# A two-layer decoder trunk on one NeuronCore: the normalised x handed over in PSUM, the query remainders one unit later, the compressed softmax without clamps, the sliding values among the first score units

## The chip, the cores and the metric

The kernel runs on one core of one Trainium2 chip. The metric is the device time of one execution in microseconds (us). A core has a matrix engine (PE), a vector engine (DVE), a scalar engine (ACT), a general engine (POOL) and a queue for DMA (SP), which run side by side and wait for each other on semaphores. PE writes its results to PSUM, which has eight banks of 128 x 512 numbers of 4 bytes; DVE and ACT read and write PSUM and SBUF.

## What is computed

`x` is 512 tokens by 1024 features. Two layers run, each of four sub-layers, and every sub-layer ends in a LayerNorm, so there are eight of them (`ln` 0 to 7 in the code):

```
for i in range(2):
    x = layer_norm(DN_ALPHA * x + 0.5 * swiglu(x, ffn1_gate[i], ffn1_up[i], ffn1_down[i]))
    y = swa_mixer(x, ...) if i == 0 else nsa_mixer(x, ...)
    x = layer_norm(DN_ALPHA * x + y)
    x = layer_norm(DN_ALPHA * x + mem_cross_attention(x, mem, ...))
    x = layer_norm(DN_ALPHA * x + 0.5 * swiglu(x, ffn2_gate[i], ffn2_up[i], ffn2_down[i]))
```

`swa_mixer` is attention of 16 heads over a sliding window of 128 tokens, with a learned sink for each head. `nsa_mixer` adds three attentions, each times a gate: one over 31 compressed blocks of keys, one over selected blocks (with these sizes all of the causal past), one over a window (also all of it). In the compressed one a token that no block precedes has probability 0 everywhere:

```
s_c = einsum('bsgrd,bngd->bgrsn', q, k_cmp) - slopes * dist_c
p_c = where(valid_c, softmax(where(valid_c, s_c, NEG_INF)), 0.0)
o_cmp = einsum('bgrsn,bngd->bsgrd', p_c, v_cmp)
```

## The kernel before

**Arithmetic.** Every product is made of three matmuls on numbers split in a rounded part and a remainder: `x_hi*w_hi`, `x_lo*w_hi`, `x_hi*w_lo` (L1328 to L1330). A slab is 128 output columns of a weight: DMA brings it to `w_raw`, ACT rounds it to `w_hi` (L621), POOL takes the remainder `w_lo` (L461). There are 379 slabs in four slots, so ACT rounds slab s when PE is done with slab s-4. ACT and POOL each have one queue in program order; calls of `feed` place the slabs in it.

**The norm between two sub-layers.** `t` holds the eight chunks (128 features by 512 tokens) of the sum. For chunk j DVE subtracts the mean (`centre`, L1024), multiplies by gain and 1/std (`scale`, L1043, out to `t`), ACT adds the offset and rounds to `x_hi` (L729), and DVE takes the remainder `x_lo` from `t` and `x_hi` (`lo`, L1049). DVE's order is scale(j), lo(j-1), centre(j+1). Norms 2, 3 and 6 (`KEEPS`) leave `lo` to POOL. Meanwhile PE projects the memory for the cross attention: `FILL` gives a norm groups of one or two of these slabs, each group into one of banks 5 and 7; norms 0, 1 and 5 have five groups, the others two, three or none. After chunk j for j in `FILL_BEHIND` (by default 1, 3, 5) ACT rounds the next slabs and copies a finished group out (L700, L704), and DVE takes that group's remainder. The next sub-layer begins with `alone` (L1372: the eight `x_hi` chunks times `w_hi`) or `together`.

**The mixers.** Heads come in eight pairs p. A unit is one head's scores for one tile of 128 queries; a pair has 8 units in the sliding mixer and 17 in the other (8 selected, 1 compressed, 8 window). In one loop over the unit number n each engine does its share for the units in flight: PE the scores of unit n (L1591, L1592), some chunks of the next pair's query slab into bank 7, transposes of finished probabilities (`turn`, L1619) and the products with the values (`values`, L1658); DVE the bias and the row minimum (`biased`, L1247; for the compressed unit the chain L1222 to L1228), the reciprocals two units later (`recip`, L1195 to L1210) and copies of turned probabilities to `pf` (L1263); ACT the exponentials (L881), the other copies to `pf` (L758), and the rounding of the next pair's queries (`q_round`, L765); POOL the normalisation (L564). DVE's `q_rest` (L1125) takes the query remainders behind `q_round`, both at the unit that `q_done` names: unit 3 of a pair in the sliding mixer, in the other 13 (14 in the first pair). PE starts the scores of unit n only when `add` counts n-2 units, and a new pair only when `qlo` says that its queries' remainders are there. `turn` m is copied by ACT if `on_act(m)`, here for even m; a pair of the second mixer has 13 turns, so from pair to pair the two engines change roles.

**The start of the sliding mixer.** PE makes two key slabs, the first query slab and then the values of all four token tiles (96 matmuls of 256 columns, L1423 to L1425, banks 5 and 6), and only then the first scores.

Of the kernel before, what the change touches and what calls it, by code (L numbers as in the profile page):

```python
# [13 lines left out]
P = 128  # L14
# [13 lines left out]
MASKED = -1.0e34  # L28
SLOTS = 4
# [40 lines left out]
class Stage:  # L70


    def __init__(self, kind, layer, ln):
# [24 lines left out]
class Mixer:  # L98
# [145 lines left out]
def build(nc, io):  # L244
# [4 lines left out]
    with ExitStack() as ctx:  # L249
# [201 lines left out]
        def _(pool):  # L451
# [24 lines left out]
            def masks():  # L476
# [51 lines left out]
            def mixer(st):  # L528
# [14 lines left out]
                for n in range(M.n + 1):  # L543
# [68 lines left out]
        def _(act):  # L612
# [77 lines left out]
            def norm(st):  # L690
# [32 lines left out]
                for j in range(KC):  # L723
# [4 lines left out]
                    else:  # L728
                        act.activation(x_hi[:, j, :], t[:, j, :], ACT.Identity, bias=b).then_inc(xhi_ready, 1)  # L729
# [44 lines left out]
            def mixer(st):  # L774
                z, M = st.sem, mixers[st.kind]
                sl = st.slab
                if st.kind == "swa":
                    feed(sl["v1"])
                    for c in range(2):
                        act.wait_ge(slab_done, sl[f"ks{c}"] + 1)  # L780
                        for half in range(2):
# [45 lines left out]
                act.wait_ge(dist_ready, 4)  # L827
                for n in range(M.end):
# [5 lines left out]
                    if st.kind == "nsa" and n in TOKENS:  # L834
                        values_nsa(st, TOKENS[n])
# [3 lines left out]
                    p = M.q_done(n)  # L839
                    if p is not None:  # L840
# [99 lines left out]
        def _(dve):  # L940
# [80 lines left out]
            def norm(st):  # L1021
# [16 lines left out]
                def scale(j):  # L1038
# [4 lines left out]
                    dve.scalar_tensor_tensor(out=t[:, j, :], in0=t[:, j, :], scalar=lng[:, st.ln, j:j + 1],  # L1043
# [879 lines left out]
```

## Time and profile before

| | us |
|---|---|
| median of 3 runs | 2307.63 (2306.52 to 2309.23) |
| the profiled execution | 2303.9 |
| its span in the trace | 2302.1 |
| PE busy in the span | 2243.1 |
| DVE, ACT, POOL busy | 732.5, 840.6, 1122.6 |

All times of the trace count from the start of the span. A row of the timeline is: start in us, duration in us, engine, line, operation with output<-input, count, and in brackets how long the engine had been idle before it and what ended that. DMA, ACT and DVE have large idle shares and are not what sets the time. The trace has its granted PE clock at 1.00 (2.4 GHz) nearly everywhere and at 0.50 (1.2 GHz) in a few short stretches.

### The profile page before, as it was taken

The numbers are of one execution on the slowest core, as the hardware profiler recorded it, in microseconds if no ns is written. First come the engines' busy times: TensorE is split into PE (matmuls) and PEld (weight loads), VectorE is DVE, ScalarE is ACT, GpSimd is POOL, SyncE is SP. The second block draws the span as 40 slices with busy tenths as digits, with TensorE's granted clock in tenths as the row PEclk, the third lists the DMA queues.
The fourth block names the chain that finished last, engine by engine and source line by source line (L and its number), as shares of the span: only waits on it lengthen the run. The fifth ranks groups of instructions, "written<-read, shape, count | busy, mean of one in ns | idle before, by whom it ended". The sixth has DMA issues, their size and how long they took to land.

```text
span 2302.1 us, 27948 instructions
## 1 busy us (share of the span) xinstructions
PE 2243.1 (97%) x10918; PEld 1846.0 (80%) x10918; DVE 732.5 (32%) x1499; ACT 840.6 (37%) x1433; POOL 1122.6 (49%) x698
## 2 busy tenths in 40 slices
PE   9999999999999999999999999999999999999998
PEld 7888888777888888888888888776667888888886
DVE  2111126564435111114211112656654444111115
ACT  3322224553435222223422223456653444222223
POOL 5454445447537444444644444444547546444443
PEclk9999999999999999999999999999999999999999
DMA  5332324213413333333333232310003313232331
GB/s 188 99 97 92 104 75 131 70 38 101 131 44 101 116 94 97 97 96 95 101 96 96 92 101 83 101 56 19 28 11 112 112 42 99 94 101 93 100 95 61
DMA packets 57874, 204.91 MB, mean 89 GB/s; under 512 B 6928, under 2 KB 7056, under 8 KB 57232
## 3 DMA queue, kind: packets, MB, share of 16 engines
q1 hardware_dynamic: 56016, 197.68, 27.3%
q10 hardware_dynamic: 1728, 5.45, 0.7%
q8 instruction: 87, 1.43, 0.3%
q14 instruction: 43, 0.35, 0.0%
HBM read 201.01 MB, written 2.10 MB: 88 GB/s over the span
## 4 chain that ended last, share of the span: by engine, by line
PE 91%; DVE 4%; ACT 2%; issue 2%; POOL 1%; DMA 0%; ACTq 0%; DVEq 0%
PE bank L1328 25%; PE bank L1330 25%; PE bank L1329 25%; PE bank L1658 2%; PE bank L1619 1%; PE bank L1591 1%; PE bank L1423 1%; DVE x_lo L1049 1%; PE bank L1358 1%; PE bank L1425 1%; PE bank L1424 1%; PE bank L1592 1%; PE bank L1347 1%; POOL w_lo L461 1%; PE bank L1355 1%
## 5 line engine op out<-in xcount | busy, mean ns | idle before, releaser
L461 POOL TENSOR_TENSOR w_lo<-w_raw,w_hi 128x1024 fp32r<-128x1024 f32 (+1 forms) x378 | 895.2, 2372 | 912.8 <-ACT w_hi L621 912.4
L1328 PE MATMUL bank<-x_hi,w_hi 128*128 128x512 f32 x1568 | 612.5, 391 | 0.0
L1329 PE MATMUL bank<-x_lo,w_hi 128*128 128x512 f32 x1568 | 610.9, 390 | 0.0
L1330 PE MATMUL bank<-x_hi,w_lo 128*128 128x512 f32 x1568 | 610.6, 389 | 0.0
L621 ACT ACTIVATE w_hi<-w_raw 128x1024 fp32r<-128x1024 f32 (+1 forms) x379 | 391.1, 1036 | 515.0 <-PE bank L1330 492.5
L1328 PE MATMUL bank<-h_hi,w_hi 128*128 128x512 f32 x960 | 379.7, 396 | 3.9 <-DVE h_lo L1270 2.8
L1330 PE MATMUL bank<-h_hi,w_lo 128*128 128x512 f32 x960 | 373.9, 389 | 0.0
L1329 PE MATMUL bank<-h_lo,w_hi 128*128 128x512 f32 x960 | 373.8, 389 | 0.0
L1330 PEld LDWEIGHTS bank<-x_hi,w_lo 128*128 128x128 f32 x1568 | 294.6, 188 | 61.8
L1329 PEld LDWEIGHTS bank<-x_lo,w_hi 128*128 128x128 f32 x1568 | 294.8, 188 | 58.5
L1328 PEld LDWEIGHTS bank<-x_hi,w_hi 128*128 128x128 f32 x1568 | 294.7, 188 | 58.4
L1098 DVE SCALAR_TENSOR_TENSOR f<-f,bank 128x512 f32<-128x512 f32 x88 | 60.6, 688 | 834.2 <-PE bank L1330 802.2
L1328 PEld LDWEIGHTS bank<-h_hi,w_hi 128*128 128x128 f32 x960 | 180.2, 188 | 47.5 <-issue 4.5
L1329 PEld LDWEIGHTS bank<-h_lo,w_hi 128*128 128x128 f32 x960 | 180.3, 188 | 37.9 <-issue 1.9
L1330 PEld LDWEIGHTS bank<-h_hi,w_lo 128*128 128x128 f32 x960 | 180.2, 188 | 37.7
L657 ACT ACTIVATE f<-bank 128x512 f32<-128x512 f32 x88 | 52.6, 597 | 361.2 <-PE bank L1330 344.6
L688 ACT ACTIVATE f<-t 128x512 f32<-128x512 f32 x64 | 40.4, 632 | 179.5 <-DVE t L999 127.4
L1247 DVE CUSTOM_DVE_ANT_0 f<-bank,dist 128x512 f32<-128x512 f32 (+3 forms) x128 | 61.2, 487 | 38.3 <-PE bank L1592 37.1
L662 ACT ACTIVATE h_hi<-f 128x512 fp32r<-128x512 f32 x88 | 54.7, 622 | 50.7 <-DVE f L1098 50.7
L881 ACT ACTIVATE t<-f,small 128x257 f32<-128x257 f32 (+5 forms) x104 | 55.1, 531 | 48.9 <-DVE small L1247 48.3
L1658 PE MATMUL bank<-pf,f 128*64 128x256 f32 (+3 forms) x384 | 61.4, 425 | 11.9 <-DVE pf L1263 6.9
L564 POOL TENSOR_SCALAR t<-t,small,gates 128x512 f32<-128x512 f32 (+3 forms) x68 | 40.8, 608 | 64.1 <-DVE small L1210 64.1
(235 smaller groups left out, 2493.0 us busy)
## 6 DMA issues: line engine op xcount, KB each, us to landing
w_raw<-w_dram SPq DMA_DIRECT2D x315, 512.0 KB, 3.5
w_raw<-w_dram SPq DMA_DIRECT2D x64, 448.0 KB, 3.2
f<-mem_dram ACTq DMA_DIRECT2D x3, 1024.0 KB, 4.9
out_dram<-t SPq DMA_DIRECT2D x8, 256.0 KB, 2.2
t<-x_dram SPq DMA_DIRECT2D x2, 512.0 KB, 6.8
f<-cmp_w_dram ACTq DMA_DIRECT2D x1, 1024.0 KB, 8.7
t<-x_dram ACTq DMA_DIRECT2D x2, 256.0 KB, 5.4
t<-x_dram ACTq DMA_DIRECT2D x1, 512.0 KB, 8.1
```

The lines of the kernel that those rows point to most:

```text
L461: pool.tensor_tensor(w_lo[:, slot(s), 0:n * P], w_raw[:, s % RAW, 0:n * P], w_hi[:, slot(s), 0:n * P].bitcast(F32), ALU.subtract).then_inc ...
L564: pool.tensor_scalar(pr, pr, rinv[:, c:c + 1], gates[:, u.i, col:col + 1], ALU.mult, ALU.mult).then_inc(z["pn"], 1)
L621: act.activation(w_hi[:, slot(s), 0:n * P], w_raw[:, s % RAW, 0:n * P], ACT.Copy).then_inc(hi_ready, 1)
L657: act.activation(gated[pair % 2], bank[UP_BANK[2 * pair % 4]][:], ACT.Silu).then_inc(z["gated"], 1)
L662: act.activation(h_hi[:, n, :], hidden[pair % 2], ACT.Copy).then_inc(z["hhi"], 1)
L881: act.activation(prob_of(u)[:, at0 - sink:at0 + u.width], scores_at(M, u)[:, 0:u.width + sink], ACT.Exp, bias=negm[:, c:c + 1], scale=-1.0 ...
L1098: dve.scalar_tensor_tensor(out=hidden[pair % 2], in0=gated[pair % 2], scalar=0.5, in1=bank[UP_BANK[(2 * pair + 1) % 4]][:], op0=ALU.mult, ...
L1247: dve.tensor_tensor_reduce(dst, src[:, 0:w], bias, -slope(h), first, ALU.add, ALU.min, negm[:, c:c + 1]).then_inc(z["add"], 1)
L1328: pe.matmul(dst, w_hi[:, slot(s), w], m_hi[:, k, :], start=k == 0, stop=False)
L1329: pe.matmul(dst, w_hi[:, slot(s), w], m_lo[:, k, :], start=False, stop=False)
L1330: last = pe.matmul(dst, w_lo[:, slot(s), w], m_hi[:, k, :], start=False, stop=k == n - 1)
L1658: last = pe.matmul(o, vals[:, b, j, rows], probs, start=begin and n < 2, stop=end and n >= len(parts) - 2, skip_group_check=True)
```

## The change

1. **x through PSUM in the full norms.** In the norms with five groups of fill (0, 1 and 5) `scale` writes to banks 6 and 4 in turn instead of `t`, and both `x_hi` and `lo` read there. `FILL_BEHIND` becomes (1, 3) for norm 1 and (1, 4) for norm 5.
2. **Queries.** `q_done` becomes `q_rounded` (ACT) and `q_rest` (DVE). In the sliding mixer ACT rounds at unit 3 as before and DVE takes the remainder at unit 4; in the first pair 5 and 6. In the other mixer they stand at 12 and 14, in the first pair at 13 and 15.
3. **`on_act`** counts turns within a pair (`m % 13 % 2 == 0`), so every pair has the same split.
4. **The compressed chain** loses both clamps (L1226, L1198). Instead the 32nd, unused column of its bias is set to -1e29. Its sum stays in PSUM, and POOL multiplies by the gates instead of DVE (L1202).
5. **Sliding values.** Tile 0 of the values stands before unit 0 and tiles 1, 2, 3 behind the scores of units 0, 1, 2, in banks 0 and 1. The next query slab's chunks move two units later in the first pair.

```diff
-FILL_BEHIND = {1: (1, 4), 5: (3, 6)}
+FILL_BEHIND = {1: (1, 3), 5: (1, 4)}
+X_BANK = (6, 4)
-TOKENS = {1: 2, 3: 3}
+TOKENS = {"swa": {0: 1, 1: 2, 2: 3}, "nsa": {1: 2, 3: 3}}
+    def x_at(self, t, bank, j):
+        return bank[X_BANK[j % 2]][:] if len(self.fill) == 5 else t[:, j, :]
...
-        return self.kind == "nsa" and m % 2 == 0
+        return self.kind == "nsa" and m % 13 % 2 == 0
...
-                at = b + k // 2 if self.kind == "swa" else b + (5 + k if p == 0 else 1 + 3 * k // 2)
+                at = (b + 2 + k // 2 if p == 0 else b + k // 2) if self.kind == "swa" else b + (5 + k if p == 0 else 1 + 3 * k // 2)
...
-            if n == self.base[p] + (3 if self.kind == "swa" else 14 if p == 0 else 13):
...
+    def q_rounded(self, n):
+        at = {"swa": (5, 3), "nsa": (13, 12)}[self.kind]
+        return [p + 1 for p in range(7) if n == self.base[p] + at[p > 0]]
+    def q_rest(self, n):
+        at = {"swa": (6, 4), "nsa": (15, 14)}[self.kind]
...
+                pool.memset(cd[:, :, NCMP:NCMP + 1], EMPTY).then_inc(dist_ready, 1)
...
                     if u.br == "cmp":
+                        pool.tensor_tensor(r8.rearrange("p (a b h) -> p a b h", a=2, b=2),
+                                           q8.rearrange("p (a b h) -> p a b h", a=2, b=2),
+                                           gates[:, :, 2 * u.p:2 * u.p + 2].rearrange("p (b a) h -> p a b h", a=2),
+                                           ALU.mult).then_inc(z["gated"], 1)
+                        pool.wait_ge(z["gated"], u.p + 1)
...
-                        act.activation(x_hi[:, j, :], t[:, j, :], ACT.Identity, bias=b).then_inc(xhi_ready, 1)
+                        act.activation(x_hi[:, j, :], st.x_at(t, bank, j), ACT.Identity, bias=b).then_inc(xhi_ready, 1)
...
-                    feed(sl["q1"])
-                    act.wait_ge(slab_done, sl["v1"] + 1)
-                    act.activation(vals[:, :, 0:2, :].rearrange("p b i d -> p i b d"),
-                                   bank[5][:].rearrange("p (i b d) -> p i b d", i=2, b=2), ACT.Copy).then_inc(z["vhi"], 1)
-                    feed(sl["q2"] + 1)
+                    feed(sl["q2"])
...
+                    if st.kind == "swa" and n == max(TOKENS["swa"]):
+                        act.wait_ge(slab_done, sl["v1"] + 1)
+                        act.activation(vals[:, :, 0:2, :].rearrange("p b i d -> p i b d"),
+                                       bank[0][:].rearrange("p (i b d) -> p i b d", i=2, b=2), ACT.Copy).then_inc(z["vhi"], 1)
...
-                    dve.scalar_tensor_tensor(out=t[:, j, :], in0=t[:, j, :], scalar=lng[:, st.ln, j:j + 1],
+                    dve.scalar_tensor_tensor(out=st.x_at(t, bank, j), in0=t[:, j, :], scalar=lng[:, st.ln, j:j + 1],
...
-                    dve.scalar_tensor_tensor(out=x_lo[:, j, :], in0=t[:, j, :], scalar=lnb[:, st.ln, j:j + 1],
+                    dve.scalar_tensor_tensor(out=x_lo[:, j, :], in0=st.x_at(t, bank, j), scalar=lnb[:, st.ln, j:j + 1],
...
-                        link(dve.tensor_scalar(s8, s8, 1.0e-30, None, ALU.max))
-                        link(dve.reciprocal(q8, s8))
+                        dve.reciprocal(q8, s8).then_inc(z["rinv"], 1)
...
-                        link(dve.tensor_tensor(sc, both[:, 1], sc, ALU.add))
+                        link(dve.tensor_tensor(both[:, 0], both[:, 1], sc, ALU.add))
-                        link(dve.tensor_scalar(m8, m8, -1.0e29, None, ALU.max))
...
-                elif u.n and st.kind == "swa":
-                    pe.wait_ge(z[("vhi", "vlo")[u.n - 1]], 1)
```

The order in three places, names as in the code; `ISA` with `dist` is `biased`, and numbers at tiles are bank numbers. First PE at the start of the sliding mixer: the end of the values' matmuls, the first scores (`mv` holds the keys, `h_hi` and `h_lo` the queries) and the first chunk of the next query slab (bank 7).

```order
L1424 MATMUL bank6<-w_hi,x_lo 128x256
L1425 MATMUL bank6<-w_lo,x_hi 128x256
L1591 MATMUL bank4<-mv,h_hi 128x256
L1592 MATMUL bank4<-mv,h_hi 128x256
L1328 MATMUL bank7<-x_hi,w_hi 128x512
```

After, the end of tile 0 of the values, the first scores, and the beginning of tile 1:

```order
L1434 MATMUL bank0<-w_lo,x_hi 128x256
L1598 MATMUL bank4<-mv,h_hi 128x256
L1599 MATMUL bank4<-mv,h_hi 128x256
L1432 MATMUL bank0<-w_hi,x_hi 128x256
L1433 MATMUL bank0<-w_hi,x_lo 128x256
```

So 72 matmuls of the values moved from ahead of the first scores to between the first three and what follows. Second, DVE at units 3 to 5 of a pair of the sliding mixer, before:

```order
L1210 RECIPROCAL small<-small 128x2
L1263 COPY pf<-bank2 128x512
L1125 SCALAR_TENSOR_TENSOR h_hi<-bank7,h_hi 64x512
L1125 SCALAR_TENSOR_TENSOR h_lo<-bank7,h_lo 64x512
L1247 ISA f2,small<-bank6,dist,nsinks 128x256
L1247 ISA small 128x1
L1247 ISA f2,small<-bank4,dist,nsinks 128x256
L1247 ISA small 128x1
L1210 RECIPROCAL small<-small 128x2
L1263 COPY pf<-bank3 128x512
```

and after:

```order
L1218 RECIPROCAL small<-small 128x2
L1269 COPY pf<-bank2 128x512
L1253 ISA f2,small<-bank6,dist,nsinks 128x256
L1253 ISA small 128x1
L1141 SCALAR_TENSOR_TENSOR h_hi<-bank7,h_hi 64x512
L1141 SCALAR_TENSOR_TENSOR h_lo<-bank7,h_lo 64x512
L1253 ISA f2,small<-bank4,dist,nsinks 128x256
L1253 ISA small 128x1
L1218 RECIPROCAL small<-small 128x2
L1269 COPY pf<-bank3 128x512
```

The bias of unit 4 went ahead of the two query remainders; both copies to `pf` stay around them. Third, DVE at units 13 to 15 of a pair of the other mixer, before:

```order
L1247 ISA f2,small<-bank6,dist 128x256
L1247 ISA small 128x1
L1125 SCALAR_TENSOR_TENSOR h_hi<-bank7,h_hi 64x512
L1125 SCALAR_TENSOR_TENSOR h_lo<-bank7,h_lo 64x512
L1247 ISA f2,small<-bank4,dist 128x256
L1247 ISA small 128x1
L1210 RECIPROCAL small<-small 128x2
L1247 ISA f2,small<-bank5,dist 128x128
```

and after:

```order
L1253 ISA f2,small<-bank6,dist 128x256
L1253 ISA small 128x1
L1253 ISA f2,small<-bank4,dist 128x256
L1253 ISA small 128x1
L1218 RECIPROCAL small<-small 128x2
L1141 SCALAR_TENSOR_TENSOR h_hi<-bank7,h_hi 64x512
L1141 SCALAR_TENSOR_TENSOR h_lo<-bank7,h_lo 64x512
L1253 ISA f2,small<-bank5,dist 128x128
```

Here unit 14's bias and a reciprocal went ahead of the remainders, while on ACT the rounding went ahead of unit 13's exponential.

## Rows read from the trace of the kernel before

**Rows 1.** The page, part 1: busy time, share of the span, instructions.

```profile
PE 2243.1 (97%) x10918; PEld 1846.0 (80%) x10918; DVE 732.5 (32%) x1499; ACT 840.6 (37%) x1433; POOL 1122.6 (49%) x698
```

**Rows 2.** Waits of PE: who waited for whom, us in total, times, longest.

```profile
PE bank L1591 <- DVE small L1247: 12.0, 13, 2.2
PE bank L1423 <- POOL w_lo L461: 9.8, 4, 4.9
PE bank L1658 <- DVE pf L1263: 6.9, 11, 1.2
PE bank L1372 <- ACT x_hi L729: 3.1, 1, 3.1
```

**Rows 3.** Windows: stretch, length, busy by engine (PE, PEld, DVE, ACT, POOL), PEclk, DMA.

```profile
397.20:400.00 2.80, 2.77 (x12) 2.31 (x13) 1.13 (x3) 1.20 (x2) 1.52 (x1) 1.00 0.69 181
434.50:436.50 2.00, 2.00 (x6) 1.61 (x6) 1.18 (x7) 1.36 (x6) 2.00 (x4) 0.50 1.02 238
1534.60:1538.00 3.40, 3.40 (x20) 2.23 (x20) 2.32 (x11) 2.99 (x10) 2.37 (x2) 0.65 0.41 148
1793.50:1796.00 2.50, 2.42 (x11) 2.45 (x12) 2.46 (x5) 0.94 (x2) 0.00 (x0) 0.50 0.62 177
```

**Rows 4.** Single lines of DVE: count, duration in ns as min/median/max, first and last start.

```profile
L1043 DVE SCALAR_TENSOR_TENSOR t<-t,lng,bank x64: 730/748/750, 375.4 to 2297.9; 128x512 f32<-128x512 f32 x64
L1125 DVE SCALAR_TENSOR_TENSOR h_hi<-bank,h_hi x16: 683/684/687, 412.9 to 1692.3; 64x512 fp32r<-64x512 f32 x16
```

**Rows 5.** Groups by line of DVE, norm 0 (377 to 398.5): count | busy, mean ns | idle.

```profile
L1049 DVE SCALAR_TENSOR_TENSOR x_lo<-t,lnb,x_hi 128x512 fp32r<-128x512 f32 x8 | 11.6, 1464 | 0.0
```

**Rows 6.** Timeline of norm 0: DVE, POOL, PE.

```profile
385.21 2.77 DVE L1049 SCALAR_TENSOR_TENSOR x_lo<-t,lnb,x_hi 128x512 fp32r<-128x512 f32 x1
385.03 5.21 POOL L461 TENSOR_TENSOR w_lo<-w_raw,w_hi 128x1024 fp32r<-128x1024 f32 x2 [3.92 <-ACT w_hi L621]
397.23 0.50 PE L1372 MATMUL bank<-x_hi,w_hi 128*128 128x512 f32 x1 [3.10 <-ACT x_hi L729]
```

**Rows 7.** Timeline of norms 1 and 5: ACT's rounding, and PE behind it.

```profile
587.54 1.99 ACT L621 ACTIVATE w_hi<-w_raw 128x1024 fp32r<-128x1024 f32 x2
593.98 0.55 PE L1423 MATMUL bank<-w_hi,ra 128*128 128x256 f32 x1 [2.90 <-POOL w_lo L461]
...
1787.21 1.99 ACT L621 ACTIVATE w_hi<-w_raw 128x1024 fp32r<-128x1024 f32 x2
1793.58 0.55 PE L1423 MATMUL bank<-w_hi,ra 128*128 128x256 f32 x1 [4.88 <-POOL w_lo L461]
```

**Rows 8.** Timeline of PE in the first pair of the sliding mixer.

```profile
433.15 0.48 PE L1591 MATMUL bank<-mv,h_lo 128*128 128x128 f32 x1 [2.24 <-DVE small L1247]
```

**Rows 9.** Timeline of a later pair of the sliding mixer, DVE and PE.

```profile
480.38 0.69 DVE L1263 COPY pf<-bank 128x512 f32<-128x512 f32 x1 [1.26 <-PE bank L1619]
...
483.09 0.33 PE L1591 MATMUL bank<-mv,h_lo 128*128 128x128 f32 x1 [0.67 <-DVE small L1247]
...
484.25 0.62 PE L1658 MATMUL bank<-pf,f 128*64 128x256 f32 x3 [0.48 <-DVE pf L1263]
```

**Rows 10.** Timeline of the other mixer's first pair: DVE, POOL, PE.

```profile
1531.08 2.38 DVE L1198 TENSOR_SCALAR small<-small 128x8 f32<-128x8 f32 x1
1531.07 2.36 POOL L461 TENSOR_TENSOR w_lo<-w_raw,w_hi 128x1024 fp32r<-128x1024 f32 x1
1534.60 0.44 PE L1658 MATMUL bank<-pf,f 128*64 128x128 f32 x4 [2.06 <-issue]
```

**Rows 11.** Timeline of two later pairs of the other mixer: PE, ACT, DVE.

```profile
1618.93 0.65 PE L1658 MATMUL bank<-pf,f 128*64 128x512 f32 x2 [1.16 <-DVE pf L1263]
...
1640.25 0.58 ACT L765 ACTIVATE h_hi<-bank 64x512 fp32r<-64x512 f32 x1
1640.86 0.68 DVE L1125 SCALAR_TENSOR_TENSOR h_hi<-bank,h_hi 64x512 fp32r<-64x512 f32 x1 [1.21 <-ACT h_hi L765]
1644.05 0.65 PE L1658 MATMUL bank<-pf,f 128*64 128x512 f32 x2 [0.31 <-ACT pf L758]
```

More of the change, by code:

```diff
@@ L28 @@
 MASKED = -1.0e34
+EMPTY = -1.0e29
 SLOTS = 4
@@ L198, in q_chunks @@
         return out
-    def q_done(self, n):
-        for p in range(7):
-            if n == self.base[p] + (3 if self.kind == "swa" else 14 if p == 0 else 13):
-                return p + 1
-        return None
+    def q_rounded(self, n):
[3 more added lines that the diff above has]
+        at = {"swa": (6, 4), "nsa": (15, 14)}[self.kind]
+        return [p + 1 for p in range(7) if n == self.base[p] + at[p > 0]]
 def kv_order(kind):
@@ L838, in mixer @@
                     turned(st, M, n)
-                    p = M.q_done(n)
-                    if p is not None:
+                    for p in M.q_rounded(n):
                         act.wait_ge(slab_done, sl[f"q{p}"] + 1)
@@ L1149, in mixer @@
                     q_rest(st, M, 0, bank[FIRST_BANK[2]])
-                    dve.wait_ge(slab_done, st.slab["v1"] + 1)
-                    dve.tensor_copy(vals[:, :, 2:4, :].rearrange("p b i d -> p i b d"),
-                                    bank[6][:].rearrange("p (i b d) -> p i b d", i=2, b=2)).then_inc(z["vlo"], 1)
                 else:
@@ L1252, in mixer @@
                         biased(M.units[n])
-                    if st.kind == "nsa" and n - 3 in TOKENS:
-                        gate(TOKENS[n - 3])
+                    if st.kind == "nsa" and n - 3 in TOKENS["nsa"]:
+                        gate(TOKENS["nsa"][n - 3])
                     if 2 <= n < M.n + 2:
@@ L1263, in mixer @@
                             dve.tensor_copy(pf[:, tn.m % 4, 0:w], bank[M.t_bank(tn.m)][:, 0:w]).then_inc(z["td"], 1)
-                    p = M.q_done(n)
-                    if p is not None:
+                    if st.kind == "swa" and n == max(TOKENS["swa"]):
+                        dve.wait_ge(slab_done, st.slab["v1"] + 1)
+                        dve.tensor_copy(vals[:, :, 2:4, :].rearrange("p b i d -> p i b d"),
+                                        bank[1][:].rearrange("p (i b d) -> p i b d", i=2, b=2)).then_inc(z["vlo"], 1)
+                    for p in M.q_rest(n):
                         q_rest(st, M, p, bank[Q_BANK])
@@ L1669, in mixer @@
                     wait_lo(pe, sl["v1"])
-                    for i in range(NT):
-                        b = bank[(5, 6)[i // 2]][:, 256 * (i % 2):256 * (i % 2) + 256]
-                        last = token_major([sl["v0"], sl["v1"]], b, i, x_hi, x_lo, 256)
-                    last.then_inc(slab_done, 2)
+                    tokens(st, 0)
                 else:
@@ L1704, in mixer @@
                         scores(st, M, M.units[n])
-                    if st.kind == "nsa" and n in TOKENS:
-                        tokens(st, TOKENS[n])
+                    if n in TOKENS[st.kind]:
+                        tokens(st, TOKENS[st.kind][n])
                     for p, k in M.q_chunks(n):
@@ L1732, in tokens @@
                 sl = st.slab
+                if st.kind == "swa":
+                    last = token_major([sl["v0"], sl["v1"]], bank[k // 2][:, 256 * (k % 2):256 * (k % 2) + 256], k, x_hi, x_lo,
+                                       256)
+                    if k == NT - 1:
+                        last.then_inc(slab_done, 2)
+                    return
                 last = token_major([sl["vs"], sl["vw"], sl["gl"]], bank[(7, 0, 1, 2)[k]][:, 0:384], NT - 1 - k, x_hi, x_lo,
```

19 lines of the change are left out of this document (7 added, 12 removed).

## The prediction

> **What bounds the kernel.** The page first: PE is busy for 2243.1 of 2302.1 us [rows 1], so at most 59 us can be won by removing waits, and some 14 of them lie at the start, the end, in the other norms and at the mixers' ends, which the change leaves alone. No engine but PE is near its limit; DVE, ACT and POOL matter only where PE stands still for them. So the second view is the list of PE's own waits [rows 2]: for the scores behind DVE's bias 12.0 us in 13 waits, for the fill slabs in the norms behind POOL's remainders 9.8 in 4, for value products behind copies to `pf` 6.9 in 11, and one of 3.1 for the last `x_hi`. The third view is the granted clock in windows [rows 3]: behind some waits it stands at 0.50 (1.2 GHz). Behind waits of 2.05 [rows 10], 2.24 [rows 8] and 4.88 [rows 7] it fell, behind one of 3.10 [rows 6] it did not (1.00 from 397.2 on), so a wait near 2 us may or may not bring the low clock. A low stretch costs half its length in matmuls.
>
> **Part 1, x through PSUM.** Every `lo` of the full norms reads two tiles of SBUF. In norm 0 the eight take 1464 ns in the mean [rows 5], and the one of 2.77 us lies inside POOL's 5.21 us for two slabs [rows 6]: it waits for POOL. DVE instructions of the same kind with one input from PSUM never take more than 750 ns (`scale`, 64 times) or 687 (`q_rest`) [rows 4], though POOL works half the time. The change gives `lo` a PSUM input, so I take 0.75 for each. Norm 0 then has 8 x (1.46 - 0.75) = 5.7 us less on DVE. PE waits there 3.10 for the last `x_hi` [rows 6]. Counting the chain again (scale, lo, centre, about 2.1 us a chunk, plus ACT's two roundings where it has to wait for a slot) the last `x_hi` comes near 392.9, about 1 us before PE asks for it: **-3.3** with 0.2 from the remainder of a fill group that DVE then has ready. Next late there is POOL's remainder of the first key slab, near 388, which leaves room.
>
> In norms 1 and 5 PE waits 2.90 and 4.88 us for POOL [rows 7], and POOL for ACT, which rounds the pair of slabs only behind `x_hi` of chunk 4 (norm 1, at 587.54) and chunk 3 (norm 5, at 1787.21). Their slots were free at 584.3 and 1783.0, when PE had ended the group before. `FILL_BEHIND` asks for them after chunks 3 and 1, and without DVE's stalls these chunks are done in time. So in norm 1 ACT rounds at 584.3, POOL is done at 1.1 + 4.8 later, 590.2, when PE ends the group in between; of 2.90 and a wait of 0.84 before it some 0.4 is left: -3.3, and the low clock behind it (2.9 us long, half lost) goes: -1.4, **-4.6** with rounding down. In norm 5 ACT rounds at 1783.0, POOL is done at 1788.9 where PE asks at 1788.7: -4.6, and the low clock (0.50 at 1793.5 to 1796 [rows 3], 4.7 us of it in all) gives 2.2: **-6.8**. Next late is `x_hi` of chunk 7, near 593.0 and 1796.3, 3 and 1 us before PE needs it. What hides the new reads and writes in banks 4 and 6 is that `together` and `alone` write them only after the last `x_lo`.
>
> One page speaks against this part. The Trainium skill ("VectorE: DVE Perf Modes", the section on the TRN2 errata) gives a VectorE instruction 58 fixed cycles from SBUF and 120 from PSUM; at its 0.96 GHz that is 65 ns more, 1.6 us over 24 `lo`, estimated from that page. The trace does not agree: 0.69 us with a PSUM input against 0.75 [rows 4], though over half the partitions.
>
> **Part 5, the sliding mixer's start.** Before, the scores of the first nine units come within 11 us, and PE stands 2.24 us for DVE's bias behind `q_rest` [rows 8]; the clock is 0.50 after it [rows 3]. After, three units have 2.9 us of value matmuls between them, so ACT's table load, its exponentials and the biases are long done. The chunks of the next query slab end at unit 5, ACT rounds them (2 x 0.6) and DVE takes the remainders (2 x 0.7), and the scores of unit 8 wait for these: about 1.4 us instead of 2.2. That is -0.8, and -1.6 for a low stretch of 3.4 us that ends: **-2.4**. The first query remainders are ready 0.7 us before tile 0 of the values ends, so unit 0 does not wait. If the low clock stays, it is -0.8.
>
> **Part 2 in the sliding mixer.** Here the step costs. In each later pair, PE's value products wait for the copy of unit 5 [rows 9]. Before that copy DVE does, without a pause: copy of unit 3 (at 480.38), two remainders, bias 4, bias 5, reciprocal, copy; PE goes on at 484.25. After, bias 4 stands behind the first copy, and its scores end only at 481.6, 0.5 us after the copy, since PE has value products ahead of them. DVE idles for that and does the same work afterwards: 484.25 becomes 484.8. PE's wait of 0.67 for unit 7's scores goes, but only into the wait for the copy. Six pairs have it: 6 x 0.53 = **+3.2**. The bounds are 0, if something else in that chain has slack that I don't see, and 6 x 0.7.
>
> **Parts 2, 3 and 4 in the other mixer.** First pair: both clamps wait for POOL, one of them 2.38 us beside a remainder of 2.36 [rows 10]; behind it the copy comes late, PE waits 2.05, and the clock is 0.65 in the mean over the next 3.4 us [rows 3]. The clamps go; the reductions and reciprocals that stay lie in the same trace at their usual length. But now `q_rest` stands at unit 15 behind a copy that waits for PE's turn of that unit: the next pair's scores wait some 2.0 us. Balance, worked out from 1534.60 to the value products after the first scores of the next pair, which took 8.6 us with the wait and take 3.9 + 2.0 + 1.0 now: **-1.7**. If the clock falls behind that wait too, for which the rows of 2.05 and 2.24 speak and the one of 3.10 doesn't, it is 0.
>
> Later pairs: at the border to the next pair PE waits for bias 14 behind `q_rest`, which itself waited 1.21 us for ACT's rounding [rows 11]. After that it waits for the copies of turns 14 and 15. Where DVE had turn 14 and ACT turn 15, the four waits are 0.2, 0.2, 0.9 and 1.16; where it was the other way round, 1.0 and 0.31 [rows 11]. The change gives every pair the second split. It puts the rounding behind exponential 12, so it starts at 1639.76 instead of 1640.25, and bias 14 no longer queues. DVE ends the remainders at 1641.8, just when PE ends unit 16; ACT ends its copy at 1642.4, DVE the other at 1642.7. PE's value products go from 1644.05 to 1642.95: -1.1 in three pairs. In the other three it is 2.5 - 0.2 = 2.3, and 0.4 in the last: 3.3 + 6.9 + 0.4 = **-10.6**. POOL's extra multiply by the gates has no row; the nearest are 0.17 for it on DVE and 0.6 for the 256-wide one behind it, and its user on PE comes 9 us later, so 0. Were it not covered, 8 x 0.6 would be +4.8.
>
> **Sum.** -3.3 - 4.6 - 6.8 - 2.4 + 3.2 - 1.7 - 10.6 = -26.2. The profiled execution of 2303.9 (span 2302.1) becomes 2277.7; on the median of 2307.6, 3.7 above it, **2281.4**.
>
> **The rivals.** (A) The hand-over doesn't free DVE: `lo` still waits for POOL. Against it speaks that 80 instructions with a PSUM input show no such wait [rows 4]. Norm 0 gives nothing, norms 1 and 5 keep what the earlier rounding brings (2.2 + 1.4, 4.2 + 2.2 less some stalls, about 9): sum -20.5, 2287. By the page's 65 ns it would be 1.6 more.
> (B) The merged wait in the sliding pairs, 0.67 + 0.48 + 0.53 = 1.7, brings the low clock in each: 6 x 1.7 = +10.2, 2291.6. For it: the clock fell behind 2.05. Against: it did not behind 3.10, nor behind 1.4.
> (C) In the second mixer the border wait only changes its cause, because the copies on ACT come later than I counted behind the rounding. Then only the equal split helps, 3 x 1.2 + 0.4 = 4: -19.6, 2288.
> (D) Slower: the late `q_rest` is a loss at every border. In the second mixer it holds up DVE's copy of turn 15 as it does in the first, +0.53 in place of the gain, and the wait grows over the point where the clock falls. Then the mixers give -2.4 + 3.2 - 1.7 + 3.2 and 12 x 1.7 = 20.4, the norms -14.7: +8, 2315.6. It decides from waits of about 2 us at all twelve borders; the two places in the trace with such waits lost the clock each time.
>
> **How the numbers follow.** Forecast 0.65, (A) 0.07, (B) 0.11, (C) 0.12, (D) 0.05. All but (D) are faster by more than 4.6 us (0.2%, about what a measurement of this kernel tells from no change); I give no change 0.02 out of the forecast's unknowns. The forecast alone spans 2277 (no loss in the sliding pairs, then 2278) to 2286 (the low clock back in both first pairs, +3.3). The range runs from 2275 to 2293: it takes in A, B and C.
>
> **What would show it.** In the changed profile: `x_lo` of the full norms at 0.7 to 0.8 us each and no wait of 3.1 before `alone`; PE's waits for POOL in norms 1 and 5 under 0.5; clock 1.00 in all three norms; the value products of each sliding pair behind one wait near 1.7 where two of 0.67 and 0.48 stood; no DVE instruction of 1.5 to 2.4 in the compressed chain; the borders of the second mixer's pairs under 0.4, except the first near 2.0. The sum is wrong if sliding pairs don't grow from 12.5 us, or if the second mixer's don't shrink to about 24.0 each where they now take 25.1 and 26.3 in turn.

## The result, and the profile after

The changed kernel takes 2283.91 us (median of 4 runs, 2281.93 to 2285.78), the kernel before 2307.16 beside it (4 runs, 2306.52 to 2309.23): a ratio of 0.9898 (95%: 0.988 to 0.9915), so it takes 1.0% less time. The forecast was 2281.4, the range 2275 to 2293. The profiled execution took 2284.9, with a span of 2283.1. Its page, part 1, answers [rows 1]:

```profile
PE 2242.0 (98%) x10918; PEld 1846.9 (81%) x10918; DVE 708.8 (31%) x1471; ACT 843.4 (37%) x1437; POOL 1121.9 (49%) x707
```

PE does the same 10918 matmuls in about the same busy time (1.1 us less). The span is 19.0 us shorter, and PE's idle time in it fell from 59.0 to 41.1 us, by 17.9. PE's waits, as in [rows 2] (total, times, longest):

```profile
PE bank L1665 <- DVE pf L1269: 12.3, 7, 2.0
PE bank L1598 <- issue: 3.6, 2, 2.1
...
PE bank L1432 <- POOL w_lo L472: 1.9, 3, 1.1
```

L1665 is now the products with the values, L1598 the scores, L1432 the fill and the sliding values. `issue` means that the profile names nothing that ended the wait; by the order of the code the two long ones at L1598, each ahead of a second pair's first scores, are for the query remainders. The 12.0 us for the bias, the 3.1 for `x_hi` and most of the 9.8 for POOL have gone; what stands for `pf` has grown from 6.9 to 12.3, nearly all of it six waits of 1.99 in the sliding pairs. No DVE instruction of the compressed chain takes over 1.2 us now, where the two clamps took 1.5 and 2.4. The single lines of `lo` (min/median/max in ns) belong beside [rows 4, 5]; the second row is norm 4, which still goes through `t`:

```profile
L1065 DVE SCALAR_TENSOR_TENSOR x_lo<-bank,lnb,x_hi x24: 744/746/751, 378.9 to 1783.9; 128x512 fp32r<-128x512 f32 x24
L1065 DVE SCALAR_TENSOR_TENSOR x_lo<-t,lnb,x_hi x8: 737/747/2181, 1465.3 to 1480.1; 128x512 fp32r<-128x512 f32 x8
```

The timeline (start, duration, then in brackets the idle time ahead and its cause) shows, from above: the products of `alone` in norm 0, all eight without the wait of [rows 6], the first sliding pair [rows 8], four later ones [rows 9], norm 1 [rows 7], the second mixer's first scores, its first border [rows 10] and two later ones [rows 11], norm 5 [rows 7].

```profile
393.20 2.03 PE L1381 MATMUL bank<-x_hi,w_hi 128*128 128x512 f32 x8
...
430.39 0.36 PE L1598 MATMUL bank<-mv,h_hi 128*128 128x256 f32 x1 [1.53 <-issue]
...
442.53 1.63 PE L1665 MATMUL bank<-pf,f 128*64 128x256 f32 x8 [1.99 <-DVE pf L1269]
...
457.28 1.09 PE L1665 MATMUL bank<-pf,f 128*64 128x256 f32 x8 [1.99 <-DVE pf L1269]
...
470.44 1.98 PE L1665 MATMUL bank<-pf,f 128*64 128x256 f32 x8 [1.99 <-DVE pf L1269]
...
485.10 1.08 PE L1665 MATMUL bank<-pf,f 128*64 128x256 f32 x8 [1.99 <-DVE pf L1269]
...
586.79 0.36 PE L1432 MATMUL bank<-w_hi,ra 128*128 128x256 f32 x1 [0.41 <-POOL w_lo L472]
...
1512.11 0.39 PE L1598 MATMUL bank<-mv,h_hi 128*128 128x512 f32 x1
...
1538.30 0.49 PE L1598 MATMUL bank<-mv,h_hi 128*128 128x512 f32 x1 [2.10 <-issue]
...
1563.56 0.47 PE L1598 MATMUL bank<-mv,h_hi 128*128 128x512 f32 x1
...
1611.16 0.47 PE L1598 MATMUL bank<-mv,h_hi 128*128 128x512 f32 x1
...
1776.73 0.36 PE L1432 MATMUL bank<-w_hi,ra 128*128 128x256 f32 x1 [0.35 <-POOL w_lo L472]
```

Last the granted clock in windows (columns as in [rows 3]; the seventh figure without brackets, ahead of the DMA share, is PEclk), at five places where it fell:

```profile
442.50:446.00 3.50, 3.47 (x14) 2.31 (x15) 1.47 (x9) 1.23 (x5) 1.58 (x3) 0.56 0.19 74
469.80:473.50 3.70, 3.06 (x12) 1.92 (x13) 1.72 (x9) 1.35 (x6) 2.18 (x4) 0.56 0.27 109
1470.00:1473.40 3.40, 3.40 (x10) 2.63 (x9) 3.37 (x7) 0.92 (x2) 0.00 (x0) 0.55 0.55 151
1501.20:1504.50 3.30, 3.04 (x10) 3.04 (x10) 0.00 (x0) 1.09 (x3) 0.21 (x1) 0.50 0.53 154
1538.30:1542.00 3.70, 3.70 (x9) 1.49 (x10) 1.00 (x5) 1.58 (x5) 1.09 (x2) 0.54 0.21 83
```

The third and the fourth lie behind norm 4, at the start of the second mixer, which no part of the change touches. At the same two places the clock of the kernel before was at its full level:

```profile
1473.00:1476.00 3.00, 3.00 (x14) 2.23 (x13) 2.96 (x6) 0.76 (x2) 0.00 (x0) 1.00 0.41 164
1503.00:1506.00 3.00, 3.00 (x18) 3.00 (x19) 0.00 (x0) 0.72 (x3) 0.00 (x0) 1.00 0.54 178
```

To compare kernels I cut the profiled executions at one landmark, the first matmul with `ones` in which PE sums up `t` for a norm's mean. "First mixer" runs from norm 0 to norm 1 and holds norm 0 and the sliding mixer, "norm 1" from there to norm 2, "second mixer" from norm 4 to norm 5 (with norm 4), "norm 5" from there to norm 6. Behind the slash stand the stretches of low clock in the stage, a long one counted as two.

| kernel | time, us | first mixer | norm 1 | second mixer | norm 5 |
|---|---|---|---|---|---|
| before | 2303.9 (profile) | 198.8 / 1 | 149.0 / 1 | 309.6 / 1 | 150.8 / 2 |
| changed | 2284.9 (profile) | 199.4 / 2 | 144.1 / 0 | 300.1 / 3 | 144.1 / 0 |
| e3_psum_only | 2296.2 | 193.2 / 0 | 144.8 / 0 | 311.0 / 1 | 150.1 / 2 |
| e4_fill_only | 2300.7 | 201.5 / 3 | 146.4 / 0 | 309.5 / 1 | 146.6 / 0 |
| e2_part1 | 2292.7 median | 194.9 / 1 | 144.1 / 0 | 312.5 / 3 | 144.1 / 0 |
| e1_rest3 | 2276.9 median | 192.6 / 0 | 144.1 / 0 | 299.0 / 2 | 144.1 / 0 |
| e6_swalate | 2313.7 median | 207.3 / 4 | 148.9 / 1 | 309.6 / 1 | 150.8 / 2 |
| e5_clamps | 2308.2 | 200.4 / 2 | 149.0 / 1 | 310.1 / 2 | 150.6 / 2 |
| e5_onact | 2304.1 | 200.4 / 2 | 148.9 / 1 | 305.9 / 1 | 150.9 / 2 |
| e7_nsaq | 2302.1 | 201.5 / 3 | 149.2 / 1 | 303.9 / 2 | 150.7 / 2 |
| e9_nsaq_onact | 2296.2 | 200.4 / 2 | 149.1 / 1 | 298.6 / 1 | 151.1 / 2 |
| e8_best | 2273.5 median | 192.5 / 0 | 144.1 / 0 | 294.6 / 0 | 144.1 / 0 |

One low stretch is worth up to 1.7 us: e2_part1 and e3_psum_only have the same first mixer but for one, 194.9 against 193.2. At other places it costs less. Behind the four waits of 1.99 where the clock fell (two in the changed kernel, two in e6_swalate) the pair takes 14.66 to 14.76 us instead of 13.17, so 1.5 to 1.6. At the start of the second mixer, from the landmark of norm 4 to the first scores, it is 82.4 to 82.5 us in the eight profiles without a low stretch, 83.8 and 84.1 in e7_nsaq and e1_rest3 with one, and 85.2 in e2_part1 and the changed kernel with two: 1.4 to 1.6 each, 2.7 for two.

### The profile page after: what moved, and what is told of

Read it like the earlier page. It is cut to its first block, busy times and chain, and to the rows that moved or that the text cites. A ratio compares the mean times of both kernels' runs of the same rounds, so it can differ in the third digit from the quotient of the medians.

```text
span 2283.1 us, 27932 instructions
## 1 busy us (share of the span) xinstructions
PE 2242.0 (98%) x10918; PEld 1846.9 (81%) x10918; DVE 708.8 (31%) x1471; ACT 843.4 (37%) x1437; POOL 1121.9 (49%) x707
## 3 DMA queue, kind: packets, MB, share of 16 engines
q8 instruction: 87, 1.43, 0.3%
## 4 chain that ended last, share of the span: by engine, by line
PE 94%; DVE 2%; issue 2%; ACT 1%; POOL 1%; DMA 0%; ACTq 0%; DVEq 0%
PE bank L1337 26%; PE bank L1339 26%; PE bank L1338 26%; PE bank L1665 2%; PE bank L1626 1%; PE bank L1598 1%; PE bank L1599 1%; PE bank L1432 1%; PE bank L1433 1%; PE bank L1434 1%; PE bank L1367 1%; PE bank L1356 1%; POOL w_lo L472 1%; PE bank L1364 1%; PE bank L1371 0%
## 5 line engine op out<-in xcount | busy, mean ns | idle before, releaser
L1665 PE MATMUL bank<-pf,f 128*64 128x256 f32 (+3 forms) x384 | 63.1, 435 | 12.5 <-DVE pf L1269 12.3
```

Of the source, the lines that this page charges most:

```text
L1665: last = pe.matmul(o, vals[:, b, j, rows], probs, start=begin and n < 2, stop=end and n >= len(parts) - 2, skip_group_check=True)
```

## Experiments

### Part 1 whole, and its two halves

e2_part1 is the kernel before with the hand-over in PSUM and the new `FILL_BEHIND`; e3_psum_only has the first of these edits, e4_fill_only the second.

```diff
+        return bank[X_BANK[j % 2]][:] if len(self.fill) == 5 else t[:, j, :]
-FILL_BEHIND = {1: (1, 4), 5: (3, 6)}
+FILL_BEHIND = {1: (1, 3), 5: (1, 4)}
```

> The kernel before with part 1 alone (x through PSUM in the full norms and the earlier rounding of fill slabs). My theory: -3.3 us in norm 0, -4.6 in norm 1, -6.8 in norm 5, the rest of the kernel as before: 2307.2 - 14.7 = 2292.5 us, with x_lo at 0.7 to 0.8 us each and no granted clock of 0.50 in these norms. Rival: part of what the three norms gain in the changed kernel is due to other parts (the clock, or work that arrives shifted from the mixers); then norm 1 or norm 5 gains less here than there.

> The kernel before with x through PSUM in the full norms, and the rounding of the fill slabs left where it was. My theory: norm 0 gains 3.3 us. In norm 1 the chunk that the rounding stands behind (4) is done 2 us earlier without DVE's stalls, which gives most of the 4.6, 4. In norm 5 it stands behind chunk 3, which only one stall of 0.25 us held up, so PE's wait of 4.88 becomes 4.3 and the clock still falls: -0.6. Sum -8, 2299. Rival: the hand-over through PSUM alone gives all, -14.7 (the places of the rounding are idle), or nothing in norms 1 and 5 (-3.3).

> The kernel before with the rounding of the fill slabs moved ahead (behind chunks 1 and 3 in norm 1, 1 and 4 in norm 5), and x in SBUF as before. My theory: norm 0 unchanged with its wait of 3.1. Norm 1: the rounding starts when chunk 3 is done, 585.3 instead of 587.5, so the wait of 2.90 falls to about 0.7: -2.2, and -1.4 if the clock then stays up. Norm 5: the rounding starts at 1783.0, the wait of 4.88 goes to 0.7 or less and the clock stays up: -6.3. Sum -9 to -10, 2298. Rival: the earlier rounding puts POOL's remainders beside more of DVE's x_lo, the stalls eat the gain, and less than half of it, 4, is left.

Measured: 2292.73 for the whole (4 runs, ratio 0.994, 0.9925 to 0.9955, beside a median of 2306.29), 2296.21 and 2300.69 in one run each. DVE's group in norm 0 (count, busy, mean ns), first e3_psum_only, then e4_fill_only:

```profile
L1054 DVE SCALAR_TENSOR_TENSOR x_lo<-bank,lnb,x_hi 128x512 fp32r<-128x512 f32 x8 | 6.0, 745 | 0.1
```

```profile
L1049 DVE SCALAR_TENSOR_TENSOR x_lo<-t,lnb,x_hi 128x512 fp32r<-128x512 f32 x8 | 11.7, 1466 | 0.0
```

So it is the PSUM input, and nothing else of the change, that frees `lo` of POOL; with it goes PE's wait of 3.10 in norm 0. In norms 1 and 5 the halves are not a plain sum. Timeline of e3_psum_only, norms 1 and 5:

```profile
586.89 0.36 PE L1428 MATMUL bank<-w_hi,ra 128*128 128x256 f32 x1 [0.54 <-POOL w_lo L466]
...
1785.82 0.55 PE L1428 MATMUL bank<-w_hi,ra 128*128 128x256 f32 x1 [4.15 <-POOL w_lo L466]
```

and of e4_fill_only, norm 0 and norm 5 (L1066 is DVE's remainder of a fill group):

```profile
398.23 0.79 PE L1372 MATMUL bank<-x_hi,w_hi 128*128 128x512 f32 x1 [3.10 <-ACT x_hi L729]
...
1790.50 0.36 PE L1423 MATMUL bank<-w_hi,ra 128*128 128x256 f32 x1 [0.77 <-POOL w_lo L461]
1798.28 0.39 PE L1328 MATMUL bank<-ra,w_hi 128*128 128x256 f32 x1 [1.80 <-DVE mv L1066]
```

In norm 1 the hand-over alone takes 4.1 of the 4.8 us: DVE is at chunk 4 in time, and the earlier rounding has little left to give. In norm 5 it takes 0.6 alone, since ACT still rounds behind chunk 3; the new `FILL_BEHIND` takes 4.2 alone and then PE waits 1.80 for DVE, which had stood at a `lo` of 2.78 us (at 1794.25) beside POOL's 5.18 for two slabs; together they take 6.7. Of the earlier rounding alone 2.2 to 3.6 us were expected in norm 1 and 6.3 in norm 5; it gave 2.5 and 4.2. So the stalls eat a part of its gain, as the rival said, but 6.7 us of the 9 to 10 are left, where the rival left 4. Its 2300.69 also holds three low stretches in the first mixer, where the profile of before has one. For e2_part1 the rival was that other parts of the change had helped in these norms. It is excluded: norms 1 and 5 take 144.1 us each in e2_part1 as in the changed kernel.

### The sliding mixer's remainders: put back, and moved alone

e1_rest3 is the changed kernel with one number back; e6_swalate is the kernel before with that one move.

```diff
-        at = {"swa": (6, 4), "nsa": (15, 14)}[self.kind]
+        at = {"swa": (6, 3), "nsa": (15, 14)}[self.kind]
```

> The changed kernel with one number put back: from the second pair of the sliding mixer on, DVE takes the query remainders at unit 3 again, not 4. My theory: the later place costs PE 0.63 us in each of six pairs (pairs of 13.17 us instead of 12.54) and makes one wait of 1.99 out of two of 0.67 and 0.48. So this kernel is 3.8 us faster than the changed one by the waits, 2280 us, and up to 3.4 more where the granted clock had fallen behind the waits of 1.99; PE's longest wait in these pairs is under 0.8 us and the clock there is 1.00. Rival: the 1.99 come from the values moved among the first units or from another part, and the place of the remainders changes nothing; then it stays at 2284 with waits of 1.99.

> The kernel before, and only the sliding mixer's later pairs take their query remainders at unit 4 instead of 3. Theory: this one move makes the six longer pairs of the changed kernel; the two waits of 0.67 and 0.48 become one of 1.99 and each pair grows by 0.63: +3.8. The clock falls behind some of them (in the changed kernel behind 2 of 6), 1.7 us each: +3.4. Together 2306.3 + 7.2 = 2313.5, 2310 without a fall. Rival: the longer pairs come from the values' new places or from the mixer's start; then the pairs stay at 12.54 us and the time at 2306.

Measured: 2276.90 (4 runs, 0.9873, 0.9857 to 0.989), 7.0 under the changed kernel (6.1 if each is measured from the kernel before that ran beside it, 2306.29 and 2307.16); and 2313.69 (10 runs, 2310.8 to 2314.68; 1.0027, 1.0017 to 1.0036), 6.8 over the kernel before, where 7.2 were expected. The rival for e6_swalate, that the long pairs come from the values' new places, is excluded. e1_rest3 has the two short waits of [rows 9] back:

```profile
453.02 0.33 PE L1598 MATMUL bank<-mv,h_lo 128*128 128x128 f32 x1 [0.66 <-DVE small L1253]
454.17 1.08 PE L1665 MATMUL bank<-pf,f 128*64 128x256 f32 x8 [0.48 <-DVE pf L1269]
```

e6_swalate has one of 1.99 in each of the six pairs; behind the first the clock stayed up, behind the second it fell (timeline, then windows):

```profile
450.17 1.08 PE L1659 MATMUL bank<-pf,f 128*64 128x256 f32 x8 [1.99 <-DVE pf L1265]
463.33 1.98 PE L1659 MATMUL bank<-pf,f 128*64 128x256 f32 x8 [1.99 <-DVE pf L1265]
```

```profile
450.20:453.40 3.20, 3.20 (x20) 2.42 (x21) 1.40 (x9) 1.82 (x7) 1.52 (x3) 1.00 0.19 72
463.70:467.00 3.30, 3.30 (x14) 2.06 (x11) 1.06 (x7) 0.88 (x5) 1.18 (x3) 0.54 0.07 29
```

DVE there, in the same pair of e6_swalate:

```profile
445.66 0.69 DVE L1265 COPY pf<-bank 128x512 f32<-128x512 f32 x1 [1.24 <-PE bank L1620]
446.90 0.48 DVE L1249 CUSTOM_DVE_ANT_0 f<-bank,dist,nsinks 128x256 f32<-128x256 f32 x1 [0.55 <-PE bank L1593]
...
447.43 0.68 DVE L1127 SCALAR_TENSOR_TENSOR h_hi<-bank,h_hi 64x512 fp32r<-64x512 f32 x1
...
449.35 0.67 DVE L1265 COPY pf<-bank 128x512 f32<-128x512 f32 x1
```

This is the loss as the prediction told it: 0.55 us in which DVE stands for bias 4's scores with the remainders queued behind it. The two kernels agree on the price: six pairs at 0.63 and two low stretches at 1.5 make 6.8.

### The second mixer, part by part

e5_clamps has part 4 alone on the kernel before, e5_onact part 3, e7_nsaq the later pairs' new units of part 2, e9_nsaq_onact the last two together.

```diff
+                pool.memset(cd[:, :, NCMP:NCMP + 1], EMPTY).then_inc(dist_ready, 1)
-                        link(dve.tensor_scalar(s8, s8, 1.0e-30, None, ALU.max))
-                        link(dve.tensor_scalar(m8, m8, -1.0e29, None, ALU.max))
```

```diff
-        return self.kind == "nsa" and m % 2 == 0
+        return self.kind == "nsa" and m % 13 % 2 == 0
```

```diff
+    def q_rounded(self, n):
+        at = {"swa": (3, 3), "nsa": (14, 12)}[self.kind]
+    def q_rest(self, n):
+        at = {"swa": (3, 3), "nsa": (14, 14)}[self.kind]
```

> The kernel before, and only the compressed chain changed: no clamps, the 32nd column's bias at -1e29, the gates multiplied on POOL. Theory: only the 2.05 us in the first pair go (no clamp waits for POOL any more), with the low clock behind them (1.7); the border behind, which waited 0.42 at the low clock and 1.57 in e3_psum_only at the full one, waits 1.6: -2.6 against the profiled execution before, 2301.3 to 2303.7. Rival: POOL's multiply by the gates holds up the products with the compressed values in every pair: +4.8, 2308 to 2311.

> The kernel before, and only the turns counted within a pair, so that ACT and DVE split the copies the same way in every pair of the second mixer. Theory: the three borders with waits of 0.2, 0.2, 0.92 and 1.16 become like the others (1.01 and 0.31), 1.2 less each, and 0.4 in the last: -3.9, near 2302.4. Rival: the split matters only together with the earlier rounding, the border still waits as before: 2306.

> The kernel before, and only the later pairs of the second mixer round their queries at unit 12 and take the remainders at unit 14 (13 and 13 before). Theory: the pairs that had the waits 1.01 and 0.31 lose 1.1 each, as in the changed kernel; in the pairs with DVE's copy behind the remainders the scores' wait goes too but the products still wait for that copy, about 1.0 less each: -6, near 2298 against a profiled execution of 2303.9 and a median of 2306.9. Rival: without the equal split the earlier rounding gives nothing in three of the pairs: -3.3, 2301 to 2304.

> e7_nsaq and e5_onact together on the kernel before, nothing else. Theory: the two add up to the later pairs of the changed kernel, 23.8 us each and borders of 0.15: -10.6 as forecast, 2293 on the profiled execution of 2303.9, 2296 on the median. Rival: the changed kernel needs the clamps' removal for its short pairs (DVE's load); then the pairs stay above 24.5 and the time is 2298 or more.

Measured, one run each: 2308.24, 2304.07, 2302.11 and 2296.18. Single times can't tell a few microseconds here (the kernel before itself ran from 2303.9 to 2309.5), so the stage and its waits decide. Against 309.6 the second mixer takes 310.1, 305.9, 303.9 and 298.6 us. That is -3.7 for the equal split (expected -3.9), -5.8 for the new units with one low stretch more (at 1506), or -7.1 without its 1.4 (expected -6, rival -3.3), and -11.0 for both, with as many low stretches as before: they add up, and the rival that needs the clamps' removal is wrong. Timeline of e7_nsaq, a border of the kind that waited 0.92 and 1.16, and of e9_nsaq_onact:

```profile
1570.35 0.47 PE L1592 MATMUL bank<-mv,h_hi 128*128 128x512 f32 x1 [0.31 <-DVE h_lo L1127]
1571.83 1.08 PE L1659 MATMUL bank<-pf,f 128*64 128x512 f32 x4 [0.56 <-ACT pf L761]
```

```profile
1590.96 0.47 PE L1592 MATMUL bank<-mv,h_hi 128*128 128x512 f32 x1
```

The clamps alone left the stage as long as it was (310.1 against 309.6), and their execution, expected at 2301.3 to 2303.7, took 2308.2. The gain is there, though, and low stretches took it away. From the first scores of the first pair to those of the second it is 25.7 us, where the kernel before takes 28.0. The wait of 2.05 went, and the next one, at the border, is 1.62 where it was 0.25 (the first row is of the kernel before, the others of e5_clamps):

```profile
1512.16 0.39 PE L1591 MATMUL bank<-mv,h_hi 128*128 128x512 f32 x1
```

```profile
1516.17 0.39 PE L1592 MATMUL bank<-mv,h_hi 128*128 128x512 f32 x1
...
1541.88 0.47 PE L1592 MATMUL bank<-mv,h_hi 128*128 128x512 f32 x1 [1.62 <-issue]
```

```profile
1543.50:1546.50 3.00, 3.00 (x9) 1.64 (x6) 0.84 (x5) 1.21 (x4) 0.69 (x2) 0.50 0.00 0
```

The clock fell behind that wait, and the second pair took 26.8 us instead of 25.2. It fell once more at 1570, at a wait of 1.17 that the kernel before has as well, and the third pair took 27.4 instead of 26.0. So -2.3 (expected -2.6), then +1.6 and +1.4. The other 4 us between the two executions lie ahead of this stage, in the start and the first mixer. The wait of 1.6 was forecast, the clock that stays up was not. The rival, POOL's multiply held up in every pair, is not what happened: no wait for it stands in the list, and the pairs without a low stretch are no longer than before.

### A version that beats both

e8_best is e1_rest3 with the second mixer's first pair at unit 14.

```diff
-        at = {"swa": (6, 4), "nsa": (15, 14)}[self.kind]
+        at = {"swa": (6, 3), "nsa": (14, 14)}[self.kind]
```

> The changed kernel with the sliding mixer's remainders back at unit 3 (as in e1_rest3, 2276.9) and, in the first pair of the other mixer, at unit 14 instead of 15. Theory: in e1_rest3 the next pair's scores wait 2.10 us at 1528.00 for remainders that DVE takes only behind bias 15 and the copy of turn 15; at unit 14 they start when ACT's rounding ends, DVE is through bias 15 about 1.2 us earlier, the wait becomes 0.9, and the low clock behind it (1531.0 to 1534.4, 1.7 us) does not come: 2276.9 - 1.2 - 1.7 = 2274.0. Rival: the wait only moves to the value products behind the copy of turn 15, which now queues behind the remainders: 2276 to 2277.

Measured: 2273.48 (2273.22 to 2274.26; ratio 0.9851, 0.9837 to 0.9866, to the kernel before at 2306.91 over 13 runs). The border, and the clock behind it:

```profile
1528.07 0.47 PE L1598 MATMUL bank<-mv,h_hi 128*128 128x512 f32 x1 [0.65 <-issue]
```

```profile
1528.10:1532.00 3.90, 3.84 (x18) 2.41 (x19) 2.71 (x12) 2.75 (x9) 2.60 (x5) 1.00 0.39 139
```

The wait went from 2.10 to 0.65, under the 0.9 expected, and the low clock with it. The rival, the wait moving on to the copy of turn 15, would have given 2276 or more. In this execution the clock stayed up until the last norm; the kernel's own spread is 1.0 us over 4 runs, where the kernel before has 5.4 over 13.

## Why the prediction was right, and where its terms were off

The forecast for the profiled execution was 2277.7; it took 2284.9. Step by step:

**Part 1** was right in all three norms. Norm 0: `lo` takes 746 ns where 1464 stood and the wait of 3.10 is gone. From the transposes of 1/std to the first product behind `alone` it is 22.5 us instead of 26.5 (374.73 to 401.22 before, 376.21 to 398.70 now), so -4.0 where I had -3.3: PE's idle time there fell by 3.34, and its busy time by 0.66, which the sum left out. Norm 1: -4.8 against -4.6. Norm 5: -6.7 against -6.8. Rival (A) fell: of 24 `lo` with a PSUM input none takes over 751 ns, while one of the eight that still read `t` takes 2181. That one starts at 1467.35, beside a remainder of POOL of 2.38 us from 1466.61. The Trainium skill ("SBUF — State Buffer", "Who interferes with whom") says that a VectorE instruction with two SBUF inputs contends with a GpSimd instruction that reads SBUF; these rows agree. On the other rule, which spoke against this part (the Trainium skill, "VectorE: DVE Perf Modes", the TRN2 errata: 62 fixed cycles more from PSUM, an estimate of 65 ns), the measurement decides: the same instruction on the same 128 x 512 has a median of 747 ns from SBUF and 746 from PSUM. Nothing of the 1.6 us is there. The prediction's own row against that rule, 0.69 us with a PSUM input against 0.75, showed nothing: `scale`, the instruction of 0.75, reads a PSUM bank as well [rows 4].

**Part 5.** The wait is 1.53 us instead of 2.24 (forecast 1.4) and the clock stayed up behind it in the changed kernel, in e1_rest3 and in e8_best: right. What the first mixer gained beyond norm 0 and lost in the later pairs leaves some -2.2 for it, forecast -2.4.

**Part 2 in the sliding mixer.** The mechanism and the sign were right, the term was too small: the six pairs go from 12.54 to 13.17 us, +0.63 each and +3.8 for +3.2. The merged wait is 1.99 us, not 1.7: PE's waits in a pair grow by 0.84, but it stands still only once, and its busy time in the pair falls from 11.4 to 11.2. What I left out is that 1.99 lies between my forecast and rival (B): the clock fell behind two of six, and in e6_swalate behind two of six as well. That is +3.1 in this execution, about a third of (B)'s 10.2. So the step cost some 7 us and not 3.2, as e1_rest3 (-7.0) and e6_swalate (+6.8) both show. I gave (B) as all six or none; a share of them should have stood in the forecast.

**The second mixer.** First pair: from its first scores to those of the second pair it took 28.0 us and takes 26.2, -1.8 where I had -1.7. The new wait is 2.10 (forecast 2.0). The clock did fall behind it, which I had put at no gain in all; the second pair takes 25.3 us instead of 23.8, so 1.5 of the 1.8 is lost again. Later pairs: 23.80 us where I had 24.0, borders of 0.15 without exception. e9_nsaq_onact puts the two causes at -11.0, against -10.6. Its pairs take 23.92, so the changed kernel has another 0.12 a pair, -0.9 over the seven, which I had at nothing. By elimination it is the shorter compressed chain; no experiment shows this by itself, and in e5_clamps, with the old waits at the borders, every second pair is shorter by 0.1 at most. The whole stage, 309.63 to 300.08, is -9.55 with two low stretches at its start that the kernel before hasn't (2.7), so -12.25 without them; take off 11.0 and 0.9, and the first pair is left with -0.3, low stretch included. Rivals (C) and (D) fell: no later border has a wait over 0.15.

**Clock where nothing changed.** Of the 7.2 us between 2277.7 and 2284.9, 4.2 are low stretches at places that the change does not touch: at waits of 1.41 and 1.13 in the second layer (at 1470 and 1501, 2.7) and one in the kernel's first 13 us (1.5). The rest is +3.1 for the two in the sliding pairs, +0.6 for these pairs' size, -0.7 for norm 0, -0.2 for norms 1 and 5, +0.2 for part 5, and in the second mixer -1.3 for the later pairs and +1.4 for the first, mostly the low stretch behind its wait; the sum is 7.3, and 0.1 is rounding. I took the profiled execution of before as a typical one with 3.7 us beside it. It was a lucky one: in norm 0 PE waits 3.10 us in every version with the old norm, and behind it the clock stayed up in the profile of before [rows 3] but fell in the six others (e4_fill_only, e5_clamps, e5_onact, e6_swalate, e7_nsaq, e9_nsaq_onact). Its start was the shortest of all twelve profiles too: 339.0 us to the landmark of norm 0, where the others take 340.0 to 341.4. These two would make up most of the 3.7. Part 1 takes the first of them out of the median, though not out of the pair of profiles. That would explain why the median came closer (2283.9 against 2281.4) than the profile; it isn't shown for the timed runs. So a part of the agreement is luck: the chance in the base and the low stretches that the sum left out work against each other.

Left open: e1_rest3 is 7.0 under the changed kernel, of which the pairs' size is 3.8; that the rest is the clock is shown for the profiled executions, not for each timed run. No experiment changed the start of the sliding mixer alone, so part 5's share is what the other terms leave. In the second mixer e8_best is 4.35 under e1_rest3: 1.5 before the first scores, for a low stretch at the wait of 1.13 that fell by chance in one and not in the other, and 2.8 over the first two pairs, which is the shorter wait (1.45) and the low stretch behind it (1.4).

## What to carry to other kernels

Where VectorE instructions with two SBUF inputs run beside a GpSimd that reads SBUF and banks are free, hand one input over in PSUM: it cost nothing here and made all 24 durations even (744 to 751 ns). Before merging two short waits into one, or moving a step behind another engine's product, look at what the new wait's length does to the clock: two of 0.67 and 0.48 cost their own time, one of 1.99 cost in a third of its places another 1.5 us. And before a profile is used as the base of a sum, count its low stretches against those of other executions of the same waits, or the change will be given what chance gave.

## What the runs showed of the hardware

Whether the granted clock falls to its lower level (1.2 GHz) at a wait differs here from one execution to the next, even for the same wait. Over the profiled executions of all twelve kernels, it fell during or right behind the wait of 4.89 in norm 5 in six of six, 2.90 in norm 1 in six of six, 3.10 in norm 0 in six of seven, 2.24 in the first sliding pair in eight of nine, 2.05 in the second mixer in seven of eight, and 2.10 there in two of two. At 1.99 it fell in four of twelve, at 1.53 in none of three, at the 1.41 to 1.43 of norm 4 in two of twelve, at two other waits of 1.41 and 1.42 in none of 24, and at 1.13 ahead of the second mixer's values in four of twelve. So the waits of 2.05 and more nearly always cost the clock. Among the shorter ones the length alone doesn't say how often; what else decides is not shown.

A low stretch doesn't always cost its 1.4 to 1.7 us. In e3_psum_only the clock stayed up behind the wait of 2.06, and then the next wait, at the border, is 1.57 us:

```profile
1526.19 0.87 PE L1663 MATMUL bank<-pf,f 128*64 128x128 f32 x8 [2.06 <-issue]
...
1531.76 0.47 PE L1596 MATMUL bank<-mv,h_hi 128*128 128x512 f32 x1 [1.57 <-issue]
```

In the kernel before it was 0.25 there, behind the slow stretch of [rows 3]:

```profile
1540.18 0.47 PE L1591 MATMUL bank<-mv,h_hi 128*128 128x512 f32 x1 [0.25 <-issue]
```

From the first scores of the first pair to these it is 28.0 us in both kernels. PE had only come to the wait earlier: with the low stretch or without it, what it waits for was ready at the same time, so the slow PE in front of them cost nothing.
